# Hybrid encoder layer on Trainium2: the projection's last tile is turned and stored within the first attention tile

## The reference, cut to what matters

```python
h = rmsnorm(x, g_attn)
proj = h @ w_in                                  # qa, ka, va, qb, kb, vb
qa, ka, va, qb, kb, vb = jnp.split(proj, splits, axis=-1)
oa = window_sink_attention(qa, ka, va, sink_a, rel_bias)     # |q - k| <= 128, 8 heads, 2 key heads
ob = axial_qknorm_attention(qb, kb, vb, gq_b, gk_b)          # dense, normed q and k, rotary positions
mixed = jnp.concatenate([rmsnorm(oa, g_out_a), rmsnorm(ob, g_out_b)], axis=-1)
x = x + mixed @ w_out
x = x + expert_choice_moe(rmsnorm(x, g_ffn), ...)            # 16 experts
x = x + sigmoid(rmsnorm(x, g_ple) @ w_ple_gate) * (p @ w_ple_proj)
return rmsnorm(x, g_final)
```

## Time and profile before

| | |
|---|---|
| median of 3 runs | 1478.36 us (1477.36 to 1478.51) |
| the profiled execution | 1476.51 us |
| its span, first to last instruction | 1474.6 us |
| mean granted clock of PE over the span | 0.98 |
| projection's last product issued | 230.24 us |
| attention's first score | 241.37 us |
| tile 1's first score | 265.9 us |

### The profile page before, as it was taken

How to read it: one execution, slowest core, us unless ns; L and a number is a source line. 1 busy time by engine, 2 the same in 40 slices (tenths; PEclk the granted TensorE clock), 3 DMA queues, 4 the chain that set the end, 5 groups by cost and what they waited for, 6 DMA issues and landing times. The chain is left out here.

```text
span 1474.6 us, 21298 instructions
## 1 busy us (share of the span) xinstructions
PE 1406.9 (95%) x7154; PEld 989.3 (67%) x7154; DVE 923.1 (63%) x1447; ACT 717.1 (49%) x1144; POOL 190.5 (13%) x257
## 2 busy tenths in 40 slices
PE   7999997999999988799999999999999999989997
PEld 5888886566555554588888656566666666558885
DVE  5644445777777788324978668666766766743343
ACT  5444435777766777322223555444444444433332
POOL 1211110000000000001001202111221122021221
PEclk9999997999999999899999999999999999999998
DMA  9444456122222233444435877877788778762331
GB/s 352 166 153 150 149 181 230 63 70 78 107 84 96 99 134 140 146 163 136 149 108 189 303 307 266 260 271 262 246 273 263 251 258 273 240 167 110 142 128 72
DMA packets 83031, 266.79 MB, mean 181 GB/s; under 512 B 8688, under 2 KB 36976, under 8 KB 67488
## 3 DMA queue, kind: packets, MB, share of 16 engines
q1 hardware_dynamic: 74752, 238.80, 45.0%
q0 software_dynamic: 7168, 25.17, 7.4%
q10 hardware_dynamic: 1056, 2.11, 0.4%
HBM read 201.55 MB, written 66.60 MB: 182 GB/s over the span
## 5 line engine op out<-in xcount | busy, mean ns | idle before, releaser
L2149 DVE TENSOR_TENSOR edge_w_lo<-ring,edge_w_hi 128x2048 fp32r<-128x2048 f32 x95 | 218.1, 2297 | 134.0 <-ACT edge_w_hi L2086 134.0
L2086 ACT ACTIVATE edge_w_hi<-ring 128x2048 fp32r<-128x2048 f32 x94 | 180.3, 1918 | 184.2 <-PE moe_p_g L2294 105.3
L1789 PE MATMUL mix_p_big<-kept_out_w,mix_m_hi 128*128 128x512 f32 x384 | 126.2, 411 | 5.6 <-DVE mix_x L1613 3.0
L1163 DVE TENSOR_REDUCE attend_ntop<-attend_p_s 128x1 f32<-128x1024 f32 (+1 forms) x96 | 100.2, 1044 | 49.4 <-PE attend_p_s L969 48.6
L579 PE MATMUL proj_p_out<-proj_w_hi,proj_h_hi 128*128 128x512 f32 x288 | 116.8, 406 | 9.7 <-DVE proj_w_lo L491 8.2
L983 PEld LDWEIGHTS attend_p_t<-kept_ident_r,attend_probs_r 128*128 128x128 f32 x896 | 97.1, 141 | 38.5 <-ACT attend_probs L1101 12.1
L983 PE MATMUL attend_p_t<-kept_ident_r,attend_probs_r 128*128 128x128 f32 x896 | 107.8, 245 | 10.8 <-ACT attend_probs L1101 5.4
L2302 PE MATMUL moe_p_gu<-ring,moe_xT_r 128*64 128x512 f32 x512 | 116.9, 598 | 0.0
L579 PE MATMUL proj_p_out<-proj_w_hi,proj_h_lo 128*128 128x512 f32 x288 | 113.3, 393 | 0.0
L579 PE MATMUL proj_p_out<-proj_w_lo,proj_h_hi 128*128 128x512 f32 x288 | 113.1, 393 | 0.0
L1101 ACT ACTIVATE attend_probs<-attend_p_s,attend_ntop 128x1024 f32<-128x1024 f32 (+1 forms) x96 | 93.4, 974 | 21.8 <-DVE attend_ntop L1163 20.6
(11 more groups left out here) (274 smaller groups left out, 2968.7 us busy)
## 6 DMA issues: line engine op xcount, KB each, us to landing
ring<-in_w_gate SPq DMA_DIRECT2D x32, 1024.0 KB, 5.6
ring<-in_w_up SPq DMA_DIRECT2D x32, 1024.0 KB, 7.4
ring<-in_w_down SPq DMA_DIRECT2D x32, 1024.0 KB, 7.2
qT_d<-proj_qT SPq DMA_DIRECT2D x12, 1024.0 KB, 3.9
proj_xT<-in_xT SPq DMA_DIRECT2D x12, 512.0 KB, 4.0
proj_w_raw<-in_w_in SPq DMA_DIRECT2D x8, 768.0 KB, 6.9
proj_x<-in_x SPq DMA_DIRECT2D x12, 512.0 KB, 4.9
kT_d<-proj_kT SPq DMA_DIRECT2D x48, 128.0 KB, 2.5
```

The lines of the kernel that those rows point to most:

```text
L1163: dve.tensor_reduce(ntop[:, s, head:head + 1], p_s[:, head % 2, 0:part.T], AX.X, ALU.max, negate=True).then_inc(ntop_done, 1)
L1789: mm = pe.matmul(p_out[:, cols], m[:, s, k, :], ww[:, k, cols], start=(k == 0 and n == 0), stop=(k == KC - 1 and n == 2))
L2086: act.activation(w_hi[:, at % SPLIT], raw[:, at % RAW], ACT.Copy).then_inc(hi_made, 1)
L2149: dve.tensor_tensor(w_lo[:, at % SPLIT], raw[:, at % RAW], w_hi[:, at % SPLIT].bitcast(F32), ALU.subtract).then_inc(lo_made, 1)
```

## The change

The last tile's five rounds leave the projection. The projection's last block ends with SP's store of tile 11's values. In attention's tile 0, PE does one round (`turn_late`) after the scores of each of steps 2 to 6, into `p_o` for rounds 0, 2, 4 and into `p_ot` for rounds 1, 3. ACT copies the former and DVE the latter after their work of that step (`copy_late`), into the place of the prompt's keys and values. PE waits for the copy of two rounds before. SP stores the queries and the four pieces of the keys behind the gains' load, ahead of the load for tile 2. So that `q_hl` and `k_hl` survive in SBUF until they are turned, the order in which the projection's tiles are placed is changed. Tile 0's copies in step 10 wait for the turned stores of tiles 0 to 10 and for all values. PE gets two waits more in tile 0, before the values' first matmul (step 11) and before the turning in step 15, both on late copies.

```diff
@@ project_inputs
-            for t in range(TILES - 3, TILES):
+            for t in range(TILES - 3, TILES - 1):
                 store(t, t % 2)
+            store_v(TILES - 1, (TILES - 1) % 2)
             ahead.projected(sp, SAMPLE_TILES)
...
             step(TILES - 1, 1, last=True)
-            copy_out(TILES - 1, 1)
...
-            transpose_qk(TILES - 1, 1)
@@ AttentionAhead
+    def turned_stored(self, eng, tiles):
+
+        eng.wait_ge(self.q_stored, 16 * tiles)
+        eng.wait_ge(self.k_stored, 64 * tiles)
@@ attend
+        late_qT = ahead.kb[:].rearrange("p a (b q) -> p (a b) q", q=P)
+        late_kT = ahead.vb
...
+        LATE_STEPS = range(2, 7)
+
+        def copy_late(eng, bank, copy, i, j):
+            if is_start(i) and j in LATE_STEPS and (j - LATE_STEPS[0]) % 2 == bank:
+                r = j - LATE_STEPS[0]
+                eng.wait_ge(late_turned, r + 1)
+                copy(late_qT[:, 4 * r:4 * r + 4, :] if r < 4 else late_kT[:], (p_o, p_ot)[bank][:]).then_inc(late_copied[bank], 1)
...
             ahead.load_gains(sp)
+            last = slice((N - 1) * P, N * P)
+            ahead.turned_stored(sp, N - 1)
+            sp.wait_ge(late_copied[0], 2)
+            sp.wait_ge(late_copied[1], 2)
+            sp.dma_start(qT_d[last, :], late_qT.bitcast(F32).rearrange("p h q -> p (h q)")).then_inc(ahead.q_stored, 16)
+            sp.wait_ge(late_copied[0], 3)
+            ahead.store_keys(sp, late_kT[:], last)
...
+            def turn_late(r):
+
+                if r >= 2:
+                    pe.wait_ge(late_copied[r % 2], r // 2)
+                for b in range(4):
+                    part = ahead.q_hl[:, 4 * r + b, :, :] if r < 4 else ahead.k_hl[:, b, :, :]
+                    mm = pe.transpose((p_o, p_ot)[r % 2][:, b, :].bitcast(F32R), part.rearrange("p a d -> p (a d)"), ident_r[:])
+                mm.then_inc(late_turned, 1)
+
             def tile(part, i, s, first, last):
                 start = is_start(i)
                 for j in range(2 * HEADS):
                     scores(part, i, s, j, first, last)
+                    if start and j in LATE_STEPS:
+                        turn_late(j - LATE_STEPS[0])
...
                 if is_start(i) and head == HEADS:
-                    ahead.projected(eng, N)
+                    ahead.turned_stored(eng, N - 1)
+                    for b in range(2):
+                        eng.wait_ge(ahead.v_stored[b], 8 * N)
...
                     exponentials(part, i, s, j, first, last)
+                    copy_late(act, 0, copy, i, j)
```

More of the change, by code:

```diff
@@ L186, in project_inputs @@
         sb, sem, sems = a.sb, a.sem, a.sems
+        x_sb = sb("x", [P, 2, D])
+        xT_sb = sb("xT", [P, 2, KC, P])
+        h_hi = sb("h_hi", [P, 2, KC, P], F32R)
+        q_hl = sb("q_hl", [P, 2 * HEADS, 2, HD], F32R)
+        k_hl = sb("k_hl", [P, 2 * KV, 2, HD], F32R)
+        ahead.q_hl, ahead.k_hl = q_hl, k_hl
         w_hi = sb("w_hi", [P, KC, QKV], F32R)
@@ L192, in project_inputs @@
         by, plus = sb("by", [P, 3]), sb("plus", [P, 3])
-        x_sb = sb("x", [P, 2, D])
         cs = sb("cs", [P, TILES, 2 * HD])
@@ L198, in project_inputs @@
         rinv = sb("rinv", [P, 2, 2])
-        xT_sb = sb("xT", [P, 2, KC, P])
-        h_hi = sb("h_hi", [P, 2, KC, P], F32R)
         h_lo = sb("h_lo", [P, 2, KC, P], F32R)
@@ L211, in project_inputs @@
         rot = sb("rot", [P, QK_B])
-        q_hl = sb("q_hl", [P, 2 * HEADS, 2, HD], F32R)
-        k_hl = sb("k_hl", [P, 2 * KV, 2, HD], F32R)
         p_out = a.ps("p_out", [P, 2, QKV])
@@ L278, in load_x, with store_v @@
                 sp.dma_start(x_sb[:, s, :], x[rows, :]).then_inc(x_landed[s], 16)
-            def store(t, s):
+            def store_v(t, s):
                 row = sp.snap(t * P)
@@ L284, in store @@
                 sp.dma_start(v_d[bass.ds(row, P), :], v_sb[:, s, :]).then_inc(v_stored[s], 16)
+                return row
+            def store(t, s):
+                row = store_v(t, s)
                 sp.wait_ge(qk_copied, t * ROUNDS + 4)
@@ L289, in store @@
                 sp.sem_inc(sp_turn, 1)
[L291 to L294, removed]
+                ahead.store_keys(sp, kT[:].bitcast(F32), bass.ds(row, P))
             load_xT(0, 0)
@@ L690, in reserve, with store_keys @@
         ctx.enter_context(self.nc.sbuf_tensor("ahead", [P, (self.nc.sbuf_top - self.low) // 4], F32, side="right"))
+    def store_keys(self, sp, kT, cols):
+        for f in range(2):
+            for half in range(2):
+                sp.dma_start(self.kT_d[half * HD:(half + 1) * HD, f::2, cols], kT[f * HD:(f + 1) * HD, :, :]).then_inc(
+                    self.k_stored, 16)
+    def turned_stored(self, eng, tiles):
+        eng.wait_ge(self.q_stored, 16 * tiles)
+        eng.wait_ge(self.k_stored, 64 * tiles)
     def projected(self, sp, tiles):
@@ L800, in attend @@
         halves = sem("halves")
+        late_turned, late_copied = sem("late_turned"), sems("late_copied", 2)
         nsink_made = sem("nsink_made")
@@ L1033, in tile @@
                         lo, hi = edges(first, last)
+                        if j == HEADS + 3 and start:
+                            pe.wait_ge(late_copied[0], 3)
                         if j == HEADS + 3:
@@ L1043, in tile @@
                         pe.wait_ge(oT_out[A], i + 1)
-                        if not start:
-                            pe.wait_ge(o_made[B], i)
+                        pe.wait_ge(*((late_copied[1], 2) if start else (o_made[B], i)))
                         turn_o(A)
@@ L1196, in tile @@
                     copy_of_step(dve, 1, part, i, j, first, last, copy)
+                    copy_late(dve, 1, copy, i, j)
                     if j == 0 and not start:
```

## The result

| | before | after |
|---|---|---|
| median of 5 runs | 1478.36 us (1477.36 to 1478.71) | 1470.51 us (1468.27 to 1472.29) |
| ratio | | 0.9945, interval 0.9932 to 0.9958 |
| profiled execution, its span | 1476.51, 1474.6 | 1468.27, 1466.5 |

The change wins 7.85 us where 4.7 were forecast. The direction was right; the time lies 1.3 us under the range's lower end of 1471.8.

A forecast was written before the change was run, and what follows sets the result against it. TensorE (PE), busy 95% of the span, was taken as the bound, so time is won only where it stands still. 7.5 us removed - 2.8 added - 0 for the clock = 4.7 off: 1478.36 to 1473.7 us, range 1471.8 to 1476.4.

The forecast's parts named there:

- The removed part: Boundary from projection to attention: release moves from 241.33 to 233.8, so 7.5 us go (bounds 7.4 to 7.7).
- The added work: Tile 0's window heads: 20 transposes cost 2.5 us and the wait for copies 0.3, together 2.8 us.
- The bound from below, 1.8: Tile 0's window heads: the least the late rounds cost, 1.8 us, ACT's copies alone setting the pace, PE's rounds in gaps.
- The copies' wait: Late rounds in tile 0: PE waits for a copy standing behind ACT's exponentials, 0.3 us, added once.
- The clock: Tile 0: level falls as before and stays low about 3 us into the dense heads; term 0, kept at +-1 us.
- the prediction's own rival: Tile 0's window heads: clock stays up or returns there, late transposes making PE denser; 6.5 us off, 1471.9, chance 0.17.
- Its 0.8 for two heads: First two dense heads of tile 0: with the clock high there, each gives 0.4 us.
- (1): Tile 0's window heads: the clock stays up or returns within them; 6.5 us off, 1471.9, chance 0.17.
- (2): Tile 0's window heads: rounds and copies go one after the other, costing 5.7 us; 1.8 off, 1476.5, chance 0.13.
- (3): Tile 0's dense heads: the low clock lasts through tile 0, costing up to 6.4 us; 1480.1, chance 0.03.
- (4): Boundary: the change doesn't move the release, so only the 2.8 us are added; 1481.2, chance 0.03.
- Loads, stores, waits: Tile 0: sample keys land three microseconds early, SP finishes late stores some 14 us early, step 10's waits cost nothing.

The follow-up runs named there:

- filler: Kernel before, nothing moved, plus 20 unused transposes in steps 2 to 6 of tile 0, copied by nobody: 1477.10 us, ratio 0.9995.
- warm: Kernel after plus 12 unused 512-wide products on PE behind the projection's last product: 1469.85 us, ratio 0.9948.
- warm without copies: Kernel after plus 12 unused products behind the projection's last, with the late transposes but without their copies and waits: 1466.84 us, one profiled run.
- no rounds: Kernel after without the five late rounds and their copies, tile 10's queries and keys stored again instead: 1470.54 us, ratio 0.9950.
- no copies: Kernel after with the 20 late transposes but without their five copies and the waits on them: 1470.17 us, ratio 0.9950.
- steps 0 to 4: Kernel after with the late rounds in steps 0 to 4 instead of 2 to 6: 1470.49 us, ratio 0.9959.
- after, again: The unchanged kernel after, measured once more beside the other kernels on the same chip: 1471.12 us, ratio 0.9954.
- stores only: Kernel before with the last tile's query store and four key stores behind attention's first loads, rounds left at the boundary: 1475.91 us, ratio 0.9993.

## Why the prediction was right or wrong

**The removed part: right.** Forecast 7.5, measured 7.64. The sum let SP's path decide, 0.65 us behind its last store, with DVE close by; SP was last, 0.1 us behind DVE, and needed 0.58 us.

**The added work: mis-sized, the first step that failed.** "20 of them are 2.5 us" took the whole distance between two transposes at the low level for each of them, since PE was "the tightest engine there, with little room". The 0.125 us for each holds in two steps of filler; in the three others PE had room, and all 20 cost 1.8 us at the low level. In after the A heads paid 7.81 - 6.79 = 1.02 us in all: two rounds at 0.50, one at 0.34, the two others nothing, and the first steps, still at 2.4 GHz, gave 0.3 back. The bound from below, 1.8, failed too: it had the rounds free and all of ACT's copies paid, while the copies lay beside PE's work at the low level.

**The copies' wait: about right in after (0.21 against 0.3), wrong in kind.** At 1.2 GHz there is none; it appears at 2.4 GHz, where the rounds wait for ACT's copies.

**The clock: the second step that failed.** "After, the A heads end about 243.4 and dense scores follow in the same order, so I take the same 3 us and a term of 0." I put the level's return down to the B heads' dense scores alone, though the prediction's own rival said the rounds would tip it. The 13 traces speak with one voice: in the six with rounds that met the low level it was back 0.3 to 3.0 us before the first B head, in the five without rounds only 0.9 to 3.8 us after it, and in the two others, warm and warm without copies, it never fell. The length of the low stretch is a weaker sign: 3.4 us in after against 6.8 in no rounds, but 6.8 also in no copies and in steps 0 to 4, where it began earlier. So that the added rounds bring the level back is shown by taking them out and putting them in; by what property of them is not.

What the return gives back is 17.78 - 16.89 = 0.89 us in the B part, and all of it lies in the first B head. PE's first score of the first three B heads, before and after:

```profile
248.16 0.76 PE L968 MATMUL attend_p_s<-attend_kb,ahead_q 128*128 128x512 f32 x1
...
250.21 0.76 PE L968 MATMUL attend_p_s<-attend_kb,ahead_q 128*128 128x512 f32 x1
...
252.75 0.51 PE L968 MATMUL attend_p_s<-attend_kb,ahead_q 128*128 128x512 f32 x1 [0.79 <-ACT attend_probs L1101]
```

```profile
240.95 0.47 PE L1000 MATMUL attend_p_s<-attend_kb,ahead_q 128*128 128x512 f32 x1 [0.16 <-DVE attend_top L1202]
...
242.09 0.46 PE L1000 MATMUL attend_p_s<-attend_kb,ahead_q 128*128 128x512 f32 x1
...
244.68 0.50 PE L1000 MATMUL attend_p_s<-attend_kb,ahead_q 128*128 128x512 f32 x1 [1.30 <-ACT attend_probs L1147]
```

The first head takes 2.05 us at the low level and 1.14 at the high one. The second takes 2.54 and 2.59: there PE waits for ACT's exponentials, and a faster PE only waits longer. The prediction set the first head's low period, 2.05, beside the fourth's high one, 2.17, and so thought a low head might cost nothing; heads of the same place must be compared. Its 0.8 for two heads came near the 0.89 by luck, since one head gave it all.

**What each was worth.** The forecast's 2.8 - 0 became 1.02 - 0.89 = +0.13 in this trace, and +0.5 by the pair with and without rounds. Neither step alone leaves the range. With 1.8 for the added work and no return of the level the time would be 1478.36 - 7.64 + 1.8 = 1472.5; with the return and a price as far above after's 1.02 as 2.8 lies above 1.8, that is 2.0, it would be 1478.36 - 7.64 + 2.0 - 0.89 = 1471.8, the range's lower end. Both are estimates from the stages.

The rule of the Trainium skill that spoke for the rival ("TensorE: Matmul & The Clock Gate", section "What's actually happening": throttled is the default and activity releases it) had the better of it. The runs agree as far as the level was back before the B heads in every kernel in which PE had more work in the A heads.

**The rivals.** (1) happened, by its mechanism: the level returned within the A heads. Its price, 1471.9, was still too careful: it charged 1.8 us for the A heads where 1.0 was paid, which makes 1471.1. The 0.6 us that are left to the median of 1470.51 can't be told from chance; after, again, gave 1471.12. (2) fell: the only wait of a late round in after was 0.21 us. (3) fell: in no kernel with rounds did the level stay low into the B heads. (4) fell with the first row.

**Loads, stores, waits: right.** The keys had 2.8 us to spare where three were forecast; that is partly luck, since they landed sooner (5.1 us for the half that is needed first, against the median of 6.8) and the A heads were shorter. The waits of step 10 cost nothing in after, but stores only shows that the edit behind this is needed.

**The range and the chances.** A rival at 0.17 that the rows and a rule supported was cut in half by the range, and its price rested on the bound of 1.8. With the 1.0 us that the A heads paid and the 0.9 given back, the sum is 7.5 - 0.1 and the time 1471.0, so a range with this case in it would have had to reach below that.

## What to carry to other kernels

Work moved from a pause into a stretch next to it is not only paid there: here it brought back the high clock level in a stretch that ran at 1.2 GHz, so price it against both levels and put what it gives back into the range. A busy share near 1 doesn't show that an engine has no room: compare the steps of a loop with each other, and those that are longer than the shortest have some. A filler kernel measures it in one run. Price a clock level by the same piece of work at both levels, not by its neighbours. When stores are moved behind loads, look for waits further on that ask for "all stores": here such a wait took back 1.8 us of 3.9.

## What the runs showed of the hardware

Kernels with the same instructions up to that point lost the high clock level up to 2.4 us apart: steps 0 to 4 at 232.96, no copies at 233.25, after at 235.10 and, again, at 235.34. What decides the moment was not found.

From the end of the last engine's drain to the first score behind the block's end it took 0.26 us where SP was last, in before and in after (241.11 to 241.37, 232.88 to 233.14), and 0.27 where ACT was, in stores only (236.63 to 236.90).

Small stores issued behind large loads landed late: four stores of 128 KB took 9.3 us behind the attention's loads in after and 8.9 us in stores only, where the same four of the projection's tile before took 2.5.
